# A chunked recurrence in 64x64 quarters of the array instead of block-diagonal 128x128 products

## The reference

```python
def step(st, inp):
    r_t, w_t, k_t, v_t, a_t, b_t = inp
    sa = jnp.einsum('dbhij,dbhj->dbhi', st, a_t)
    st = st * w_t[..., None, :] + sa[..., None] * b_t[..., None, :] + v_t[..., None] * k_t[..., None, :]
    y = jnp.einsum('dbhij,dbhj->dbhi', st, r_t)
    return st, y
s0 = jnp.zeros((2, B, H, N, N), jnp.float32)
_, ys = lax.scan(step, s0, xs)
y = ys[:, 0] + ys[::-1, 1]
```

## Time and profile before

| What | us |
|---|---|
| median of three runs | 3549.57 |
| least and most | 3544.44, 3551.37 |
| profiled execution, span from the first to the last instruction | 3544.3 |
| PE busy in the span | 3418.1 |
| DVE busy | 2414.6 |
| ACT busy | 1555.8 |
| recurrence, eight pairs, 72.1 each | 576.8 |

### The profile page before, as it was taken

How to read it: one execution, slowest core, us unless ns; L and a number is a source line. 1 busy time by engine, 2 the same in 40 slices (tenths; PEclk the granted TensorE clock), 3 DMA queues, 4 the chain that set the end, 5 groups by cost and what they waited for, 6 DMA issues and landing times.

```text
span 3544.3 us, 66333 instructions
## 1 busy us (share of the span) xinstructions
PE 3418.1 (96%) x27186; PEld 3280.6 (93%) x27186; DVE 2414.6 (68%) x3244; ACT 1555.8 (44%) x1859; POOL 83.0 (2%) x156
## 2 busy tenths in 40 slices
PE   8999999999999899999999999989998999999998
PEld 8997899999989875999999999979988899999998
DVE  8776966676668797777765544565566677777545
ACT  5442444444414402554444444454445555555443
POOL 0001100000000000000000000000000000000000
PEclk9999999999999999999999999999999999999999
DMA  8658611221158654567765555535443455555554
GB/s 331 257 192 337 238 57 57 84 84 56 56 225 325 251 210 142 202 237 284 284 237 189 191 201 191 202 122 179 155 155 107 164 189 189 188 189 189 196 191 155
DMA packets 94087, 663.67 MB, mean 187 GB/s; under 512 B 10353, under 2 KB 10993, under 8 KB 15346
## 3 DMA queue, kind: packets, MB, share of 16 engines
q1 hardware_dynamic: 74736, 540.05, 42.1%
q0 software_dynamic: 14400, 104.86, 7.8%
q10 hardware_dynamic: 4802, 16.54, 1.2%
HBM read 655.12 MB, written 6.29 MB: 187 GB/s over the span
## 4 chain that ended last, share of the span: by engine, by line
PE 85%; DVE 9%; ACT 3%; DMA 2%; issue 1%; SPq 0%; ACTq 0%; DVEq 0%
PE ps L462 20%; PE ps L463 20%; PE ps L464 20%; PE ps L434 4%; PE ps L722 2%; PE ps L493 2%; PE ps L710 2%; DVE work L1824 2%; PE ps L646 2%; PE ps L647 2%; PE ps L648 2%; DMA work<-in_ada 2%; DVE ring_parts L1801 1%; PE ps L506 1%; PE ps L768 1%
## 5 line engine op out<-in xcount | busy, mean ns | idle before, releaser
L1801 DVE TENSOR_TENSOR ring_parts<-ring,ring_hi 128x1024 fp32r<-128x1024 f32 x866 | 1042.0, 1223 | 697.4 <-ACT ring_hi L1131 685.3
L1131 ACT ACTIVATE ring_hi<-ring 128x1024 fp32r<-128x1024 f32 x866 | 909.4, 1059 | 1140.8 <-PE ps L464 1087.2
L463 PE MATMUL ps<-h_lo,ring_hi 128*128 128x256 f32 x2624 | 729.2, 278 | 0.0
L462 PE MATMUL ps<-h_hi,ring_hi 128*128 128x256 f32 x2112 | 592.9, 281 | 15.8 <-DVE h_lo L1831 8.5
L464 PE MATMUL ps<-h_hi,ring_parts 128*128 128x256 f32 x2112 | 585.2, 277 | 0.0
L463 PEld LDWEIGHTS ps<-h_lo,ring_hi 128*128 128x128 f32 x2624 | 496.9, 189 | 1.4 <-issue 1.2
L462 PE MATMUL ps<-x_hi,ring_hi 128*128 128x256 f32 x1664 | 466.0, 280 | 10.3 <-DVE x_lo L1831 5.8
L463 PE MATMUL ps<-x_lo,ring_hi 128*128 128x256 f32 x1664 | 462.3, 278 | 0.0
L464 PE MATMUL ps<-x_hi,ring_parts 128*128 128x256 f32 x1664 | 460.6, 277 | 0.0
L462 PEld LDWEIGHTS ps<-h_hi,ring_hi 128*128 128x128 f32 x2112 | 396.6, 188 | 18.3 <-issue 9.8
L464 PEld LDWEIGHTS ps<-h_hi,ring_parts 128*128 128x128 f32 x2112 | 396.8, 188 | 0.0
(11 more groups left out here) (502 smaller groups left out, 6421.2 us busy)
## 6 DMA issues: line engine op xcount, KB each, us to landing
ring<-in_weights SPq DMA_DIRECT2D x511, 1024.0 KB, 4.8
work<-in_ada POOLq DMA_DIRECT2D x96, 1024.0 KB, 6.8
work<-in_c_row POOLq DMA_DIRECT2D x4, 1024.0 KB, 6.2
gate_store<-gate_out ACTq DMA_DIRECT2D x8, 512.0 KB, 2.8
work<-gate_store ACTq DMA_DIRECT2D x2, 2048.0 KB, 19.3
resid<-in_lora ACTq DMA_DIRECT2D x9, 256.0 KB, 2.6
resid<-in_x SPq DMA_DIRECT2D x4, 512.0 KB, 6.3
resid<-in_x ACTq DMA_DIRECT2D x1, 2048.0 KB, 26.9
```

The costliest lines, as they stand in the source:

```text
L462: mm(o, w_hi[:, k, cols], hi(kc), start=(kc == 0 and m % 2 == 0), stop=False, skip_group_check=True)
L463: mm(o, w_hi[:, k, cols], lo(kc), start=False, stop=False, skip_group_check=True)
L1131: A(high_ring(n)[:, 2 * (e % 2) + half, :], ring[:, n % RING, half * (SLOT // 2):(half + 1) * (SLOT // 2)], ACT.Copy)\
L1801: tt(lo, x, high_ring(n)[:, e % 4, :].bitcast(F32), ALU.subtract).then_inc(S("lo_ready"), 1)
```

## The change

The two heads' blocks are now stacked on the partitions and not block-diagonal. `AR`, `BK`, `XY`, `LS`, `ZS` hold 64 columns per block. For L, the levels, U, SA and the state a product for both heads becomes two products of 64x64, one on rows and columns 0 to 63 of the array, one on 64 to 127 (`HALVES`; SA goes to the other half of the columns). The Gram products use 64 rows and 128 columns for each head, with a bank of their own, and one mask with both triangles.

The inverse is no longer formed anew in each level: X and Y start with a product with the identity (`ident2`) in PSUM, and each level adds its product to the same bank (`start=False`). So Z is only masked, and the identity isn't added to it; Y gets its own product instead of a transpose of X. The part of U that does not depend on the state is computed for all four chunks ahead of the steps, in the bank of Y, and the steps add to it. DVE updates the state with one operation (`stt`), the decayed old state `STP` being prepared a step ahead; `SBD`, `STMP`, `AK`, `RRM` and `VV` are gone, with the clearing of the zeros on POOL and DVE. ACT copies half as many columns per matrix, in the order X, Y of one direction, then of the other, and its gate split in levels 2 and 3 comes after these four copies. The loop over the pairs is written out eight times on PE alone.

The core of the diff:

```diff
 C_ALL = [("ident", P), ("ones", P), ("eps", 4)]
-C_1 = [("bones", P), ("swap", P), ("cos", T), ("sin", T), ("reset", T), ("lvl", 2 * 6 * P), ("strict", 2 * CH),
-       ("incl", 2 * CH), ("lmask", 2 * P)]
+C_1 = [("bones", P), ("swap", P), ("cos", T), ("sin", T), ("reset", T), ("lvl", 2 * 6 * CH), ("gmask", 2 * P),
+       ("lmask", 2 * CH), ("ident2", CH)]
 C_3 = [("swap128", P), ("swap64", P), ("tri", P), ("sp_mask", TRI), ("sp_min", TRI), ("causal", TRI), ("cneg", TRI),
        ("freq", 8), ("e0", P)]
...
@@ -300,25 +301,23 @@
...
+    BK = w(at, 8, 2, CH); at += 1024
+    AR = w(at, 8, 2, CH); at += 1024
+    BKT = w(at, 8, P); at += 1024
+    GM = w(at, 2, 2, 4, P); at += 2048
+    SV = w(at, 8, 2, CH); at += 1024
     US = w(at, 2, CH); at += 128
     ST = w(at, 2, CH); at += 128
...
+    STP = w(at, 2, CH); at += 128
+    at += 4096
     EP = w(at, 2, T); at += 512
     RC, KC, NC_ = w(at, T), w(at + 256, T), w(at + 512, T); at += 768
     VD = w(at, 4, 2, CH); at += 512
     RB = w(at, T); at += 256
...
@@ -649,8 +643,7 @@
                 if u % 8 == 7:
                     ins.then_inc(S("half_used") if half == 0 else w_used, 1)
-        with pe.Fori(0, PAIRS) as i:
-            t.enter(i, sm)
+        for i in range(PAIRS):
             t.wait(S("lw_loaded"), 16)
             t.wait(S("pair_done"), 1)
             for k in range(4):
@@ -665,112 +658,115 @@
             t.wait(S("tilde_ready"), 1)
             t.wait(S("vt_read"), 1)
+            for e in range(8):
+                for h, hs in enumerate(HALVES):
+                    ins = mm(PS[hs, 4, e * CH:(e + 1) * CH], AR[hs, e, 0, :], BK[hs, e, 1 - h, :], start=True, stop=True)
+            t.give(ins, S("l_mm"))
+            for d in range(2):
+                for c in range(4):
+                    for h, hs in enumerate(HALVES):
+                        ins = mm(PS[:, 2 + 3 * d + h, c * P:(c + 1) * P], BK[hs, 4 * d + c, :, :].rearrange("p a b -> p (a b)"),
+                                 AR[hs, 4 * d + c, :, :].rearrange("p a b -> p (a b)"), start=True, stop=True)
+                t.give(ins, S("gram_mm"))
             for d in range(2):
                 if d == 1:
                     t.wait(S("l_read"), 1)
                 for c in range(4):
...
+                    ins = pe.transpose(PS[:, 7 - 3 * d, c * P:(c + 1) * P],
+                                       BK[:, 4 * d + c, :, :].rearrange("p a b -> p (a b)"), ident)
+                t.give(ins, S("bkt_mm"))
+            gate_tiles(36, 4, i)
+            t.wait(S("y_init"), 1)
+            for d in range(2):
+                t.wait(S("gram_read"), 1)
                 for c in range(4):
...
+                    for hs in HALVES:
+                        ins = mm(PS[hs, 3 + 3 * d, c * CH:(c + 1) * CH], XY[hs, d, 1, c, :], con("ident2", CH)[hs],
+                                 start=(c == 0), stop=False, skip_group_check=True)
+                t.give(ins, S("xy_mm"))
+            t.wait(S("bkt_read"), 2)
+            for d in range(2):
                 for c in range(4):
...
+                    for hs in HALVES:
+                        mm(PS[hs, 4 + 3 * d, c * CH:(c + 1) * CH], con("ident2", CH)[hs], XY[hs, d, 1, c, :],
+                           start=(c == 0), stop=False, skip_group_check=True)
             for l in range(2, 7):
                 for d in range(2):
...
+                    t.wait(S("x_init" if l == 2 else "xy_ready"), 1)
                     for c in range(4):
...
+                        for hs in HALVES:
+                            ins = mm(PS[hs, 2 + 3 * d, c * CH:(c + 1) * CH], LS[hs, d, c, :], XY[hs, d, 0, c, :],
+                                     start=True, stop=True)
                     t.give(ins, S("z_mm"))
...
                 for d in range(2):
                     t.wait(S("z_ready"), 1)
                     if l > 2:
                         t.wait(S("yt_ready"), 1)
                     for c in range(4):
...
+                        for hs in HALVES:
+                            ins = mm(PS[hs, 3 + 3 * d, c * CH:(c + 1) * CH], XY[hs, d, 1, c, :], ZS[hs, d, c, :],
+                                     start=False, stop=False, skip_group_check=True)
                     t.give(ins, S("xy_mm"))
...
+                    if l < 6:
+                        for c in range(4):
+                            for hs in HALVES:
+                                ins = mm(PS[hs, 4 + 3 * d, c * CH:(c + 1) * CH], ZS[hs, d, c, :], XY[hs, d, 1, c, :],
+                                         start=False, stop=False, skip_group_check=True)
+                        t.give(ins, S("yt_mm"))
+
+            u_of = lambda hs, d, c: PS[hs, 4 + 3 * d, c * CH:(c + 1) * CH]
+            for d in range(2):
+                for c in range(4):
+                    for h, hs in enumerate(HALVES):
+                        ins = mm(u_of(hs, d, c), GM[hs, d, h, c, 0:CH], SV[hs, 4 * d + c, h, :], start=(c == 0), stop=False,
+                                 skip_group_check=True)
+                t.give(ins, S("u_mm"))
+            y = lambda hs, c: PS[hs, 2, c * CH:(c + 1) * CH]
             for k in range(4):
...
+                if k > 0:
+                    for d in range(2):
+                        c = k if d == 0 else 3 - k
                         t.wait(S("s_ready"), 1)
...
+                        for hs in HALVES:
+                            ins = mm(u_of(hs, d, c), AR[hs, 4 * d + c, 0, :], ST[hs, d, :], start=False, stop=True,
+                                     skip_group_check=True)
+                        t.give(ins, S("u_mm"))
                 if k < 3:
                     gate_tiles(40 + 8 * k, 2, i)
                 for d in range(2):
                     c = k if d == 0 else 3 - k
+                    if k == 0:
+                        t.wait(S("xy_ready"), 1)
                     t.wait(S("u_ready"), 1)
...
+                    for h, hs in enumerate(HALVES):
+                        ins = mm(PS[HALVES[1 - h], 3 + 3 * d, 0:CH], XY[hs, d, 0, c, :], US[hs, d, :], start=True, stop=True)
+                    t.give(ins, S("sa_mm"))
                 if k < 3:
                     gate_tiles(40 + 8 * k + 2, 2, i)
...
                 if k > 0:
                     for d in range(2):
                         c = k if d == 0 else 3 - k
...
+                        for hs in HALVES:
+                            mm(y(hs, c), ST[hs, d, :], AR[hs, 4 * d + c, 1, :], start=False, stop=False, skip_group_check=True)
                 for d in range(2):
                     c = k if d == 0 else 3 - k
                     e = 4 * d + c
                     t.wait(S("sa_ready"), 1)
...
                     if k < 3:
...
+                        for h, hs in enumerate(HALVES):
+                            ins = mm(PS[hs, 3 + 3 * d, CH:2 * CH], BKT[:, e, h * CH:(h + 1) * CH], SV[:, e, h, :],
+                                     start=True, stop=True)
                         t.give(ins, S("s_mm"))
                 for d in range(2):
                     c = k if d == 0 else 3 - k
...
+                    for h, hs in enumerate(HALVES):
+                        ins = mm(y(hs, c), SV[:, 4 * d + c, h, :], GM[:, d, h, c, CH:P], start=(k == 0 and d == 0), stop=True,
+                                 skip_group_check=True)
                     if k == 3 and d == 1:
                         t.give(ins, S("y_mm"))
                 if k < 3:
                     gate_tiles(40 + 8 * k + 4, 4, i)
...
@@ -1320,20 +1313,19 @@
             half_split(gates + 2, 1, i, 4)
             for d in range(2):
                 t.wait(S("bkt_mm"), 1)
...
+                t.give(A(BKT[:, 4 * d:4 * d + 4, :].rearrange("p a b -> p (a b)"), PS[:, 7 - 3 * d, :], ACT.Copy), S("bkt_read"))
+            for d in range(2):
                 t.wait(S("xy_mm"), 1)
...
+                t.give(A(XY[:, d, 0, :, :].rearrange("p a b -> p (a b)"), PS[:, 3 + 3 * d, 0:T], ACT.Copy), S("x_init"))
             for l in range(2, 7):
                 for d in range(2):
                     t.wait(S("xy_mm"), 1)
...
+                    t.give(A(XY[:, d, 0].rearrange("p a b -> p (a b)"), PS[:, 3 + 3 * d, 0:T], ACT.Copy), S("xy_ready"))
+                    if l < 6:
                         t.wait(S("yt_mm"), 1)
...
+                        t.give(A(XY[:, d, 1].rearrange("p a b -> p (a b)"), PS[:, 4 + 3 * d, 0:T], ACT.Copy), S("yt_ready"))
+                if l in (2, 3):
+                    half_split(gates + 3, l - 2, i, 4)
             if more:
                 for n in (4, 5):
...
+            ar = AR.rearrange("p (d c) k s -> p d c k s", d=2)
+            tt(ar[:, :, :, 0, :], both(NC_), d4(EM), ALU.mult)
+            t.give(tt(ar[:, :, :, 1, :], both(RC), d4(EP), ALU.mult), S("tilde_ready"))
             step(tt(TM[:, 0, :], KD[:, 0, :], KD[:, 1, :], ALU.add))
             t.give(stt(RB, TM[:, 0, :], PP[:, 5:6], RC, ALU.mult, ALU.mult), S("rb_ready"))
             v.wait_ge(S("tilde_ready"), t.value(S("tilde_ready")))
```

(57 more changed lines are left out.)

127 lines of the change are left out of this document (19 added, 108 removed).

## The result

The changed kernel takes 3415.57 us (median of four runs, 3414.30 to 3434.81) against 3550.11 us of the kernel before beside it: ratio 0.9631, 95% interval [0.9608, 0.9655]. That is 134.5 us less where 96 were forecast; 3454 was predicted, in a range of 3380 to 3585. An execution's time lies 1.3 us above its span (3414.5 and 3413.2 in the profiled one); the 5.3 us given ahead of the prediction hold, beside that, what single executions differ by.

What follows compares the result with a forecast made beforehand. The eight pairs were taken as a queue of PE passes. Per pair, levels, preparation and steps gave -14.05 us and switches +2.1: -12.0, times eight -96, from the median 3549.57 to 3454 us, range 3380 to 3585.

Steps and rivals of the forecast that it cites:

- q: Spacing of quarter passes (64x64, one head each) on PE: taken as 0.040 us, between 0.028 and 0.056, or 0.112.
- levels: Five levels of the inverse in a pair: 18.5 us against 25.04, so -6.5 us (-10.9 at 0.028 us a pass).
- preparation: L, Gram products and starts of X and Y in a pair: 8.7 us against 9.92, so -1.2 us.
- steps: State steps 0 to 3 of a pair: together -6.35 us (-8.2 at 0.028 us a pass).
- switches: 26 changes of pass shape a pair, each 0 to 0.163 us: half taken, +2.1 us a pair (0 to 4.2).
- Gram: Gram products in a pair's preparation: 32 passes, 64 rows and 128 columns, spaced by 0.080 us, 2.56 us in all.
- step 3: Last state step of a pair, without gate tiles, so the chain counts: 2.3 us against 3.43, so -1.15 us.
- wait for the first mask: In each level, PE waits 0.11 us after z until DVE's first mask is ready at 1.39 us.
- One after the other: Rival: quarter passes run serially at 0.056 us: 3548 us (3531 to 3565 by switch cost); chance 0.22.
- Price kept: Rival: a pass costs 0.112 us whatever its size, +313 us, 3863 us; chance 0.12, including any spacing above 0.06.
- Clock: Rival: clock falls to 1.2 GHz in the levels, passes cost double (0.080 us), +123 us, 3673 us; chance 0.06.
- The opening: Sign of being wrong: the opening stretch grows because DVE's splits come late; no size given.

Runs made afterwards that it cites:

- written-out loop: The kernel before with only its PE loop over the eight pairs written out: 3551.05 us, ratio to before 1.0010.
- doubled mask: The changed kernel with a second DVE masking in each level, changing no value: 3437.07 us, ratio to before 0.9677.
- Head by head: The changed kernel with eight passes of one head, then eight of the other, in Z, X and Y of the levels: 3446.22 us, ratio to before 0.9697.
- blocks of 16: The changed kernel with the passes of a level in blocks of 16 of one head: 3498.83 us, ratio to before 0.9866.

## Why the prediction was right, and where it was off

**Bound and scope.** Right: the gain lies in the eight pairs, and 8 x 16.8 us is all of it, 15.8 of the 16.8 as passes on PE and 1.0 as waits that are gone. The written-out loop gave nothing, as forecast. One reading was wrong without effect: the last level did have transposes before (L715, levels 3 to 6), and the count of 192 passes holds with them.

**q, the mis-sized term.** I took 0.040 between 0.028 and 0.056; it is 0.0285 to 0.029, half of the 0.058 of one quarter alone: quarters of different rows and columns run fully side by side. At 0.028 the working gave levels -10.9 (measured -10.6), preparation -2.2 (-2.17) and steps -8.2 (-4.14 with the switches in them). With 0.040 the levels were short by 4.1 and the preparation by 1.0; over all parts it cost 21.3 - 14.05 = 7.25 us a pair, 58 in all. Gram, taken at 0.080, is 0.0575. The Trainium skill, page TensorEngine Tiling (Array Packing), section Tiling Modes, has different tiles loading and multiplying in parallel; 0.029 where one quarter alone takes 0.058 agrees.

**The switches.** I took half of 0.163 us; the whole was due, 0.17. Of the 26 switches of a pair 22 lie in the steps, at 0.163 that is 3.6 us: -8.2 + 3.6 = -4.6 against the measured -4.14, and step 3, below, takes 0.2 of the rest. So my steps and switches together (-6.35 + 2.1 = -4.25) came out right by two errors that cancel, which is luck. The other four belong to the preparation, and its -2.17 shows nothing of them: PE waits there for DVE's Gram masks, as forecast (the start of X, L684, takes 606.91 - 605.59 = 1.32 us for 32 passes, where L takes 1.08), so that what comes before costs nothing. The Trainium skill, page TensorEngine Tiling (Array Packing), section Tiling Modes, says that changing the tiling mode drains TensorE; the 0.17 us agrees. Both ends together, -21.3 + 4.2 = -17.1 a pair or -137 us, is close to what the runs show (-134). The middle value of q left out 58 us of the gain, that of the switch 17 us of the cost; the difference, 41, is nearly the 38 us by which the forecast fell short.

**The waits.** A wait for the first mask was forecast at 0.11 us a level; the loads wait 0.2, and a level takes 0.28 more than its passes. With faster passes Z ends sooner and DVE doesn't: the working has it too, with 0.0285 for 0.040 (Z 0.91, mask ready at 0.43 + 0.31 + 0.425 + 0.06 = 1.22). The doubled mask shows that it is on the path. ACT's four copies stay hidden, as forecast. Step 3 was put at 2.3 us and is 2.52.

**The rivals.** One after the other (3548): refuted by the spacing of 0.0285. "Head by head" and "blocks of 16" show that in the levels it would have come true in part with another order of the same passes: they cost 28 and 84 of the 86 us that no overlap would, the second in part by its waits. Price kept (3863): refuted by the same spacing. Clock (3673): it stayed at 1.00, the 2.4 GHz level, in all stages of the pair shown. The opening, named as a danger, is longer by 0.1 us a pair.

## What to carry to other kernels

Two heads' 64x64 products on opposite quarters cost half of one block-diagonal 128x128 product here, 4 x 0.029 = 0.117 us against 2 x 0.112 = 0.224, if the passes alternate between the quarters in program order, one by one. Count the changes of shape at 0.17 us each and group the small products between full ones. When PE's passes get shorter, look next for the DVE operation between them that has not, and put passes that are independent of it into its place.

## What the hardware showed unexpectedly

In these traces passes on different quarters don't start in program order: one starts three or four places ahead if its quarter is free. So n passes in a row on one quarter cost about n x 0.058 - 0.18 us before the other quarter begins; that is worked out from blocks of 8 and of 16 alone. The changed kernel shows it too, in step 3, where the program has all of L743 ahead of L751:

```profile
638.72 0.33 PE L743 MATMUL ps<-work 64*64 64x64 f32 x4 [0.21 <-DVE work L2076]
638.86 0.27 PE L751 MATMUL ps<-work 64*64 64x64 f32 x2
638.88 0.30 PE L743 MATMUL ps<-work 64*64 64x64 f32 x4
```

It need not be both rows and columns: the Gram products of the two heads share the columns and not the rows, and go at 0.0575, half of 0.112; the products of L758 share the rows and not the columns, and eight take 0.45 us, as eight quarter passes do (L732 above). What such a product costs with one head alone no run shows.
